# Ten gate blocks of each feed-forward: every second weight slab by seven block products over sums, and the feed-forward in two parts

## Chip, cores and metric

One core of a Trainium2 chip runs the whole program. The metric is the device time of one execution in microseconds, and a change counts by the ratio of the times of the kernel after and the kernel before, timed on the same chip. All numbers below are of the kernel before.

## What is computed

A sequence of 256 tokens with 2048 features (fp32) passes through a feed-forward, a token-mixing block, a second feed-forward, and two further layers. The change is in the two feed-forwards alone:

```
def _swiglu(h, w_gu, w_down):
    gate, up = jnp.split(h @ w_gu, 2, axis=-1)
    return (jax.nn.silu(gate) * up) @ w_down

x = x + 0.5 * _swiglu(_rmsnorm(x, ffn1_norm[l]), ffn1_w_gu[l], ffn1_w_down[l])
```

w_gu is 2048 x 11264 (5632 gate columns, then 5632 up columns), w_down is 5632 x 2048. The second feed-forward has the same shapes. Beside them runs the product of a 2048-vector with the 2048 x 6144 matrices w_ada of the two last layers: mod = silu(c) @ w_ada + b_ada.

## The kernel before

Weights come as **slabs**: 128 partitions x 1024 fp32 numbers (512 KB), which is two chunks of 128 rows of a weight matrix (WK = 2) by 512 of its columns (WN = 512). A product is computed to fp32 accuracy by splitting both operands into a high part (rounded to fp32r) and a low part (the rest), and adding three passes on TensorE: high x high, low tokens x high weights, high tokens x low weights. Tokens are the stationary operand (128 x 128, halves T = 0 and 1 of the 256 tokens), weights the moving one.

Each slab goes through five hands, on five queues:

1. SP issues its load into `stage`, a ring of RING = 4, once the slab four places earlier has been split.
2. ACT writes the high part into `split_slabs`, a ring of 4 (SPLIT_FFN), in slab order (`round_upto`, `rounded_part`, L1627). It waits for the load, and for `slab_done` of the slab four places earlier, whose place it takes.
3. POOL (`rest`, L880) or DVE (`slab_lo`, L2132) writes the low part, stage minus high part. The set `by_vector` says which: in a feed-forward about every second slab is DVE's.
4. PE multiplies (`wide_passes`): eight matmuls with the high part (L1088), then, after a wait for the low part, four with it (L1093), each 128 x 128 by 128 x 512. The last raises `slab_done`.
5. `slab_done` frees the place for ACT.

```
1088:  mm(ps[:, 2 * pair + T, :], stationary(kk, i)[:, T * P:(T + 1) * P], w[0][:, kk, :],
1090:  pe.wait_ge(*slab_split(n))
1093:  ins = mm(ps[:, 2 * pair + T, :], stationary(kk, 0)[:, T * P:(T + 1) * P], w[1][:, kk, :],
```

A feed-forward has 11 groups j of 16 slabs: eight for 512 gate columns, eight for the 512 up columns of the same place; then 4 groups d of 22 slabs of w_down. ACT takes the silu of the gate sums out of PSUM (L1696), DVE multiplies with the up sums (`gated`, L2172), turns the result by 32 x 32 blocks into PSUM (`turn_act`, L2186, 16 of them a group), ACT rounds it (`round_act`, L1702), and DVE writes its low part (`rest_act`, L2195). All of this is done one group behind, at fixed places q = 0 to 15 of the group.

DVE also computes the product with w_ada, 96 loads of two chunks in each feed-forward, at places `ADA_AT` between the slabs (`ada`): per load two multiply-adds over 128 x 512 (L2145 and L2149; the first of a column group is L2142), whose running sum `total` stands in PSUM, bank 5. Each eighth load ends with a transpose (L2152) and a sum (L2154).

The order on each engine is written out by hand as loops over groups and places; DVE, ACT, POOL and SP each work strictly through their own list, and meet only at semaphores.

## Time and profile before

| what | value |
|---|---|
| median of 3 runs | 3026.06 us (3023.61 to 3027.93) |
| the profiled execution, span | 3022.0 us, 46302 instructions |
| PE busy | 3001.6 us (99%), 18688 matmuls |
| DVE busy | 1983.5 us (66%) |
| ACT busy | 1449.2 us (48%) |
| POOL busy | 1326.5 us (44%) |
| first feed-forward | from 14 to 717 us of the span |
| second feed-forward | from 1447 to 2158 us of the span |

The profile gives for the profiled execution its span, from the first to the last instruction; no separate time of that execution is listed. The median of the runs is 4.1 us (0.13%) above the span. Busy time of an engine leaves out waits on semaphores, but contains the time in which an instruction that has begun is held up: that shows as a longer duration.

### The profile page before, as it was taken

The page shows a single profiled execution, that of the slowest core. Times are in us where ns is not written, and L with a number is a line of the kernel's source. Part 1 is how long each engine was busy: PE and PEld are TensorE (multiplying, and loading weights), DVE is VectorE, ACT ScalarE, POOL GpSimd, SP SyncE. Part 2 cuts the span into 40 slices and gives each one's busy share as a digit, 9 for nine tenths or more (in the row PEclk, how much of TensorE's full clock was granted, in tenths as well). Part 3 has the DMA queues.
Part 4 walks back from the last instruction along what each step waited for, and adds up shares of the span by engine and source line. Part 5 has one row for each costly group of instructions (what it writes and reads, how often), then busy time and mean ns, then how long its engine had stood idle before and what let it go on. Part 6 is the DMA issues. An engine that isn't in the chain of part 4 may idle for free.

```text
span 3022.0 us, 46302 instructions
## 1 busy us (share of the span) xinstructions
PE 3001.6 (99%) x18688; PEld 2660.7 (88%) x18688; DVE 1983.5 (66%) x2918; ACT 1449.2 (48%) x1885; POOL 1326.5 (44%) x653
## 2 busy tenths in 40 slices
PE   9999999999999999999999999999999999999998
PEld 7888888888999999998888888888899998999997
DVE  4777665664324457777566666577579866789764
ACT  6444444444657455544544444444544454544454
POOL 5455545445565555585554555444550004710013
PEclk9999999999999999999999999999999999999999
DMA  7888887886776555566688888788576546665555
GB/s 241 274 279 264 273 282 252 290 287 182 226 175 175 158 165 150 151 170 199 214 274 285 268 272 268 263 291 279 172 216 195 161 143 213 183 192 182 154 181 181
DMA packets 491662, 663.33 MB, mean 220 GB/s; under 512 B 70440, under 2 KB 278040, under 8 KB 490936
## 3 DMA queue, kind: packets, MB, share of 16 engines
q1 hardware_dynamic: 485960, 655.85, 68.5%
q0 software_dynamic: 4448, 2.94, 0.3%
q8 instruction: 147, 2.41, 0.3%
q10 hardware_dynamic: 1040, 1.58, 0.2%
q14 instruction: 67, 0.55, 0.1%
HBM read 656.06 MB, written 2.11 MB: 218 GB/s over the span
## 4 chain that ended last, share of the span: by engine, by line
PE 96%; DVE 3%; ACT 0%; issue 0%; POOL 0%; DMA 0%; DVEq 0%; ACTq 0%
PE ps L1088 37%; PE ps L952 20%; PE ps L1093 18%; PE ps L958 10%; PE ps L969 3%; PE ps L974 1%; PE ps L936 1%; DVE narrow_split_slabs L2132 1%; PE ps L1571 1%; PE ps L1350 1%; PE ps L1331 1%; DVE h_split L2089 1%; PE ps L1059 0%; DVE U L2082 0%; PE ps L1358 0%; PE ps L1388 0%
## 5 line engine op out<-in xcount | busy, mean ns | idle before, releaser
L880 POOL TENSOR_TENSOR split_slabs<-stage,split_slabs 128x1024 fp32r<-128x1024 f32 x318 | 775.4, 2439 | 1289.3 <-ACT split_slabs L1627 1289.2
L1627 ACT ACTIVATE split_slabs<-stage 128x1024 fp32r<-128x1024 f32 x592 | 627.3, 1061 | 858.7 <-PE ps L1093 790.8
L1088 PE MATMUL ps<-split_slabs,h_split 128*128 128x512 f32 x3288 | 813.1, 389 | 0.0
L1627 ACT ACTIVATE narrow_split_slabs<-stage 128x1024 fp32r<-128x1024 f32 (+1 forms) x437 | 457.7, 1051 | 611.0 <-PE ps L958 460.6
L1088 PEld LDWEIGHTS ps<-split_slabs,h_split 128*128 128x128 f32 x3288 | 616.9, 188 | 127.9
L2132 DVE TENSOR_TENSOR split_slabs<-stage,split_slabs 128x1024 fp32r<-128x1024 f32 x274 | 354.0, 1292 | 493.0 <-ACT split_slabs L1627 491.1
L952 PE MATMUL ps<-h_split,narrow_split_slabs 128*128 128x256 f32 x4928 | 620.6, 279 | 2.9 <-issue 1.9
L952 PEld LDWEIGHTS ps<-h_split,narrow_split_slabs 128*128 128x128 f32 x4928 | 586.0, 188 | 14.5 <-issue 8.7
L880 POOL TENSOR_TENSOR narrow_split_slabs<-stage,narrow_split_slabs 128x1024 fp32r<-128x1024 f32 (+1 forms) x182 | 441.2, 2434 | 317.5 <-ACT narrow_split_slabs L1627 317.1
L1093 PE MATMUL ps<-split_slabs,h_split 128*128 128x512 f32 x1644 | 439.4, 389 | 0.0
L2132 DVE TENSOR_TENSOR narrow_split_slabs<-stage,narrow_split_slabs 128x1024 fp32r<-128x1024 f32 x255 | 339.5, 1335 | 126.8 <-ACT narrow_split_slabs L1627 125.7
L1093 PEld LDWEIGHTS ps<-split_slabs,h_split 128*128 128x128 f32 x1644 | 308.6, 188 | 64.0
L1088 PE MATMUL ps<-split_slabs,act_split 128*128 128x512 f32 x1392 | 344.0, 389 | 0.0
L958 PE MATMUL ps<-h_split,narrow_split_slabs 128*128 128x256 f32 x2464 | 331.1, 277 | 0.0
L1088 PEld LDWEIGHTS ps<-split_slabs,act_split 128*128 128x128 f32 x1392 | 261.3, 188 | 54.1
L958 PEld LDWEIGHTS ps<-h_split,narrow_split_slabs 128*128 128x128 f32 x2464 | 303.7, 188 | 0.0
L1093 PE MATMUL ps<-split_slabs,act_split 128*128 128x512 f32 x696 | 186.0, 389 | 0.0
L2186 DVE STREAM_TRANSPOSE ps<-U 32x256 f32<-32x256 f32 x352 | 160.3, 455 | 4.9
L1093 PEld LDWEIGHTS ps<-split_slabs,act_split 128*128 128x128 f32 x696 | 130.7, 188 | 27.2
L2145 DVE SCALAR_TENSOR_TENSOR ps<-U,cact,ps 128x512 f32<-128x512 f32 x168 | 126.2, 751 | 14.8 <-DMA U<-in_w_ada 12.1
L2149 DVE SCALAR_TENSOR_TENSOR ps<-U,cact,ps 128x512 f32<-128x512 f32 x168 | 127.0, 756 | 6.0
L2568 DVE SCALAR_TENSOR_TENSOR U<-U,params 128x256 f32<-128x256 f32 x240 | 112.2, 509 | 0.0
(309 smaller groups left out, 2516.9 us busy)
## 6 DMA issues: line engine op xcount, KB each, us to landing
stage<-in_ffn_w_gu SPq DMA_DIRECT2D x352, 512.0 KB, 4.9
stage<-in_w_in SPq DMA_DIRECT2D x349, 512.0 KB, 3.9
U<-in_w_ada SPq DMA_DIRECT2D x192, 512.0 KB, 5.4
stage<-in_ffn_w_down SPq DMA_DIRECT2D x176, 512.0 KB, 5.1
stage<-in_w_out SPq DMA_DIRECT2D x96, 512.0 KB, 4.2
stage<-in_w_in SPq DMA_DIRECT2D x80, 128.0 KB, 2.8
stage<-in_w_branch_c SPq DMA_DIRECT2D x32, 192.0 KB, 3.5
stage<-in_cmp_w SPq DMA_DIRECT2D x8, 512.0 KB, 4.9
```

Source lines behind the costliest of these rows:

```text
L880: nc.gpsimd.tensor_tensor(slab_part(n, 1, size(n)), stage[:, n % RING, 0:size(n)], slab_part(n, 0, size(n)).bitcast(F32), ALU.subtract).th ...
L952: mm(bank[:, c * S:(c + 1) * S], w[0][:, kk, at:at + P], moving(kk, i), start=first and c == 0 and kk == 0 and i == 0, stop=False)
L958: ins = mm(bank[:, c * S:(c + 1) * S], w[1][:, kk, at:at + P], moving(kk, 0), start=False, stop=last and c == outs - 1 and kk == chunks - 1)
L969: mm(bank[:, T * W2:(T + 1) * W2], hx[:, i, KC * k + kk, T * P:(T + 1) * P], w[0][:, kk, :], start=k + T + kk + i == 0, stop=False)
L1088: mm(ps[:, 2 * pair + T, :], stationary(kk, i)[:, T * P:(T + 1) * P], w[0][:, kk, :], start=first and kk == 0 and i == 0, stop=False)
L1093: ins = mm(ps[:, 2 * pair + T, :], stationary(kk, 0)[:, T * P:(T + 1) * P], w[1][:, kk, :], start=False, stop=last and kk == WK - 1)
L1627: return fn(slab_part(n, 0, size(n)), stage[:, n % RING, 0:size(n)], ACT.Copy)
L2132: v.tensor_tensor(slab_part(n, 1), stage[:, n % RING, :], slab_part(n, 0).bitcast(F32), ALU.subtract).then_inc(lo_vec, 1)
L2145: ins = v.scalar_tensor_tensor(total, w[:, 0, :], cact[:, 2 * k:2 * k + 1], total, ALU.mult, ALU.add)
L2149: v.scalar_tensor_tensor(sums, w[:, 1, :], cact[:, 2 * k + 1:2 * k + 2], total, ALU.mult, ALU.add).then_inc(ada_load, 1)
L2186: last = v.transpose(dst[turned_rows, :, :, rows], src[rows, :, :, turned_rows])
L2568: ins = v.scalar_tensor_tensor(cy[:, c, :], src, col, cy[:, c, :], ALU.mult, ALU.add)
```

## The change

**The seven products.** In the groups j = 1 to 10 of both feed-forwards, of the eight gate slabs those with q = 1, 3, 5, 7 (STR_SLABS) are no longer multiplied directly. A slab of two chunks by 512 columns is seen as a 2 x 2 matrix of blocks of 128 x 256, the tokens of its two chunks as a 2 x 2 matrix of blocks of 128 x 128, and the product of the two is made by seven block products instead of eight (Winograd's form). Four of the seven take sums of weight blocks as the moving operand, and four take sums of token blocks as the stationary one.

- DVE (`sum_slab`) makes the weight sums: 128 x 512, then 128 x 256 twice, each from the one before, all from `stage` and `slab_sums` (which lies in the low part of the slab's place in the ring). It then also makes the low part of the three plain blocks (128 x 768).
- ACT makes two high parts: of the plain blocks (128 x 768, into the new ring `plain_split` of 2) and of the sums (128 x 1024).
- POOL makes the low part of the sums, as for any other slab.
- PE (`summed_passes`) multiplies 21 times 128 x 128 by 128 x 256, in four stretches with a wait before each, in place of 12 times 128 x 128 by 128 x 512.
- The seven products go to four PSUM banks (the gate pair and banks 4 and 5). Gate sums are therefore put together after the last slab: ACT copies a quarter (`copy_gate`, place 11), DVE adds three times and then once over 128 x 1024 (`sum_gate`, place 12), ACT takes the silu in SBUF (`silu_summed`, place 14).
- Once a feed-forward, in group 0, DVE and ACT make the token sums of the 8 chunks concerned, high and low part (`combine`, `round_combined`, `rest_combined`).

**Who makes the low parts.** In groups 1 to 10 DVE keeps two slabs of the sixteen (q = 10 and 15); the other fourteen are POOL's.

**The product with w_ada.** Its running sum moves from PSUM bank 5 to SBUF (`ada_run`), since bank 5 is taken. Six loads are placed in each of the ten groups (q = 2, 9, 11, 13, 14, 15), the remaining 36 in the down products.

**Two parts.** PARTS = ((0, 6), (6, 11)): after gate and up groups 0 to 5, the down product runs over their 24 chunks (4 groups of 12 slabs), and after groups 6 to 10 over the other 20 (4 groups of 10). x is thus updated eight times a feed-forward, not four. This halves the room for activations, which pays for the new tiles.

The core of the diff:

```
+PARTS = ((0, 6), (6, 11))
+ADA_SLABS = (2, 9, 11, 13, 14, 15)
+STR_SLABS = (1, 3, 5, 7)
...
+        by_vector -= {s + gu_at(j) + q for s in (S_F1, S_F2) for j in range(1, GU_GROUPS) for q in range(16)}
+        by_vector |= {s + gu_at(j) + q for s in (S_F1, S_F2) for j in range(1, GU_GROUPS) for q in (10, 15)}
...
+            def summed_passes(pair, n, q, first, last):
...
+                of_plain = ((tokens(0, 0), ps[:, 4, low]), (combined(3), ps[:, 2 * pair, low]), (tokens(1, 0), ps[:, 2 * pair, high]))
+                of_sums = ((combined(0), ps[:, 5, low]), (combined(1), ps[:, 5, high]), (combined(2), ps[:, 4, high]),
+                           (tokens(1, 1), ps[:, 2 * pair + 1, high]))
+                pe.wait_ge(plain_hi, nth_sum[n])
+                for k, (stationary, sums_to) in enumerate(of_plain):
+                    for i in range(2):
+                        mm(sums_to, stationary(i), whole[0][:, k, :], start=first and k == 0 and i == 0, stop=False)
+                pe.wait_ge(hi_done, nth[n])
...
+                pe.wait_ge(plain_lo, nth_sum[n])
...
+                pe.wait_ge(*slab_split(n))
...
+                    if m in nth_sum:
+                        k = nth_sum[m]
+                        act.wait_ge(*slab_loaded(m))
+                        if k > 2:
+                            act.wait_ge(slab_done, summed[k - 3] + 1)
+                        fn(plain_part(m, 0), stage[:, m % RING, STR_COLS:SLAB], ACT.Copy).then_inc(plain_hi, 1)
+                        act.wait_ge(slab_summed, k)
+                        fn(slab_part(m, 0), sums_of(m), ACT.Copy).then_inc(hi_done, 1)
...
-                w, total = u(ADA_RING, P, 2, WK, WN)[:, m % 2], ps[:, 5, :]
+                w, total = u(ADA_RING, P, 2, WK, WN)[:, m % 2], ada_run
...
+                def sum_slab(n):
+                    dve.wait_ge(*slab_loaded(n))
+                    dve.wait_ge(slab_done, before[n] + 1)
+                    whole, sums = col_blocks(stage[:, n % RING, :]), col_blocks(sums_of(n))
+                    chained(v.tensor_tensor(sums[:, 0:2, :], whole[:, 0:1, :].broadcast_to([P, 2, STR_COLS]), whole[:, 1:3, :], ALU.subtract), "sum1", n)
+                    chained(v.tensor_tensor(sums[:, 2, :], whole[:, 2, :], sums[:, 0, :], ALU.subtract), "sum2", n)
+                    v.tensor_tensor(sums[:, 3, :], whole[:, 3, :], sums[:, 2, :], ALU.subtract).then_inc(slab_summed, 1)
+                    dve.wait_ge(plain_hi, nth_sum[n])
+                    v.tensor_tensor(plain_part(n, 1), stage[:, n % RING, STR_COLS:SLAB], plain_part(n, 0).bitcast(F32), ALU.subtract
+                                    ).then_inc(plain_lo, 1)
...
+                def sum_gate(j):
+                    dve.wait_ge(gate_copied, (GU_GROUPS - 1) * f + j)
...
+                    v.tensor_tensor(u(SILU, P, TT, WN), u(SILU, P, TT, WN), ps[:, pair:pair + 2, :], ALU.add).then_inc(gate_summed, 1)
...
+                        if j > 0 and q == 12:
+                            sum_gate(j)
+                        if j == 0 and q == 11:
+                            combine()
+                        if j == 0 and q == 12:
+                            rest_combined()
...
+                for part, (j0, j1) in enumerate(PARTS):
+                    for j in range(j0, j1):
+                        gate_and_up(j)
+                    down(part)
```

How the order moves, first on PE, in the gate half of a group. Before, each slab is a row of eight matmuls with high parts and a row of four with low parts:

```order
L1088 MATMUL ps<-split_slabs,h_split 128x512 x8
L1093 MATMUL ps<-split_slabs,h_split 128x512 x4
L1088 MATMUL ps<-split_slabs,h_split 128x512 x8
L1093 MATMUL ps<-split_slabs,h_split 128x512 x4
```

After, an even slab (q = 0, 2, 4, 6) stays as it was (now L1153 and L1158), and an odd one reads:

```order
L1182 MATMUL ps<-plain_split,h_split 128x256 x2
L1182 MATMUL ps<-plain_split,combined_split 128x256 x2
L1182 MATMUL ps<-plain_split,h_split 128x256 x2
L1186 MATMUL ps<-split_slabs,combined_split 128x256 x6
L1186 MATMUL ps<-split_slabs,h_split 128x256 x2
L1189 MATMUL ps<-plain_split,h_split 128x256
L1189 MATMUL ps<-plain_split,combined_split 128x256
L1189 MATMUL ps<-plain_split,h_split 128x256
L1192 MATMUL ps<-split_slabs,combined_split 128x256 x3
L1192 MATMUL ps<-split_slabs,h_split 128x256
```

These are 14 matmuls with high parts and 7 with low parts, of half the width.

Second, on DVE, in the same half of a group, from `gated` on. Before (L2132 is a slab's low part, L2145 and L2149 are the product with w_ada, reading and writing PSUM):

```order
L2172 SCALAR_TENSOR_TENSOR U<-ps,rstd,U 128x512 x2
L2132 TENSOR_TENSOR split_slabs<-stage,split_slabs 128x1024
L2186 STREAM_TRANSPOSE ps<-U 32x2x4x32 x12
L2132 TENSOR_TENSOR split_slabs<-stage,split_slabs 128x1024
L2186 STREAM_TRANSPOSE ps<-U 32x2x4x32 x4
L2132 TENSOR_TENSOR split_slabs<-stage,split_slabs 128x1024
L2145 SCALAR_TENSOR_TENSOR ps<-U,cact,ps 128x512
L2149 SCALAR_TENSOR_TENSOR ps<-U,cact,ps 128x512
```

After (L2354 to L2358 are `sum_slab` of q = 3, 5 and, behind the first transposes, 7):

```order
L2322 SCALAR_TENSOR_TENSOR U<-ps,rstd,U 128x512 x2
L2354 TENSOR_TENSOR slab_sums<-stage 128x512
L2355 TENSOR_TENSOR slab_sums<-stage,slab_sums 128x256
L2356 TENSOR_TENSOR slab_sums<-stage,slab_sums 128x256
L2358 TENSOR_TENSOR plain_split<-stage,plain_split 128x768
L2354 TENSOR_TENSOR slab_sums<-stage 128x512
L2355 TENSOR_TENSOR slab_sums<-stage,slab_sums 128x256
L2356 TENSOR_TENSOR slab_sums<-stage,slab_sums 128x256
L2358 TENSOR_TENSOR plain_split<-stage,plain_split 128x768
L2336 STREAM_TRANSPOSE ps<-U 32x2x4x32 x8
```

The three low parts are gone from here, and each of the four odd slabs has four operations in their place. In the second half of the group the list reads, from place 9:

```order
L2295 SCALAR_TENSOR_TENSOR U<-U,cact 128x512
L2299 SCALAR_TENSOR_TENSOR U<-U,cact 128x512
L2282 TENSOR_TENSOR split_slabs<-stage,split_slabs 128x1024
L2295 SCALAR_TENSOR_TENSOR U<-U,cact 128x512
L2299 SCALAR_TENSOR_TENSOR U<-U,cact 128x512
L2345 TENSOR_TENSOR act_split<-ps,act_split 128x512 x2
L2388 TENSOR_TENSOR U<-U,ps 128x256
L2389 TENSOR_TENSOR U<-U,ps 128x2x256
L2390 TENSOR_TENSOR U<-U,ps 128x256
L2391 TENSOR_TENSOR U<-U,ps 128x1024
L2295 SCALAR_TENSOR_TENSOR U<-U,cact 128x512
L2299 SCALAR_TENSOR_TENSOR U<-U,cact 128x512
```

L2295 and L2299 are the product with w_ada, now from SBUF to SBUF; L2388 to L2391 are `sum_gate`.

## Rows read from the trace of the kernel before

**Rows 1.** The page's busy times: engine, busy us (share), instructions
```profile
PE 3001.6 (99%) x18688; PEld 2660.7 (88%) x18688; DVE 1983.5 (66%) x2918; ACT 1449.2 (48%) x1885; POOL 1326.5 (44%) x653
```
**Rows 2.** Waits, longest first (engine line <- releaser: us, times, longest), all engines
```profile
POOL split_slabs L880 <- ACT split_slabs L1627: 1289.2, 311, 235.3
ACT split_slabs L1627 <- PE ps L1093: 790.8, 517, 2.0
```
**Rows 3.** Timeline of PE, first feed-forward: start, us, engine line op operands xcount
```profile
302.43 1.98 PE L1088 MATMUL ps<-split_slabs,h_split 128*128 128x512 f32 x8
...
305.15 1.98 PE L1088 MATMUL ps<-split_slabs,h_split 128*128 128x512 f32 x8
```
**Rows 4.** Timeline of PE, token mixing, matmuls of half the width
```profile
797.34 1.98 PE L952 MATMUL ps<-h_split,narrow_split_slabs 128*128 128x256 f32 x16
...
800.06 1.98 PE L952 MATMUL ps<-h_split,narrow_split_slabs 128*128 128x256 f32 x16
```
**Rows 5.** Lines one by one: count, then duration ns min/median/max, first to last start
```profile
L880 POOL TENSOR_TENSOR split_slabs<-stage,split_slabs x318: 2357/2401/3400, 7.9 to 3003.5; 128x1024 fp32r<-128x1024 f32 x159
L2132 DVE TENSOR_TENSOR split_slabs<-stage,split_slabs x274: 1212/1226/3434, 24.2 to 3006.1; 128x1024 fp32r<-128x1024 f32 x137
L2145 DVE SCALAR_TENSOR_TENSOR ps<-U,cact,ps x168: 742/750/757, 78.2 to 2109.3; 128x512 f32<-128x512 f32 x168
L2149 DVE SCALAR_TENSOR_TENSOR ps<-U,cact,ps x168: 754/756/757, 77.3 to 2104.4; 128x512 f32<-128x512 f32 x168
L2460 DVE TENSOR_TENSOR U<-U x16: 692/1625/2194, 1301.7 to 1356.3; 128x512 f32<-128x512 f32 x16
```
**Rows 6.** The same view, operations of DVE that stay as they are
```profile
L2172 DVE SCALAR_TENSOR_TENSOR U<-ps,rstd,U x44: 737/744/753, 58.3 to 1922.5; 128x512 f32<-128x512 f32 x44
L2186 DVE STREAM_TRANSPOSE ps<-U x352: 440/456/468, 61.6 to 1936.5; 32x256 f32<-32x256 f32 x176
L2195 DVE TENSOR_TENSOR act_split<-ps,act_split x44: 680/683/686, 81.9 to 1947.9; 128x512 fp32r<-128x512 f32 x44
L2152 DVE STREAM_TRANSPOSE ps<-U x24: 727/727/728, 121.7 to 2110.8; 128x512 f32<-128x512 f32 x24
L2154 DVE TENSOR_REDUCE U<-ps x24: 691/692/693, 122.4 to 2111.6; 128x16 f32<-128x512 f32 x24
```
**Rows 7.** Timeline, ACT, DVE and POOL in a group: start, us [idle before <- releaser]
```profile
299.97 1.06 ACT L1627 ACTIVATE split_slabs<-stage 128x1024 fp32r<-128x1024 f32 x1 [0.51 <-PE ps L1093]
300.68 0.75 DVE L2145 SCALAR_TENSOR_TENSOR ps<-U,cact,ps 128x512 f32<-128x512 f32 x1
301.11 2.41 POOL L880 TENSOR_TENSOR split_slabs<-stage,split_slabs 128x1024 fp32r<-128x1024 f32 x1 [3.03 <-ACT split_slabs L1627]
301.47 0.76 DVE L2149 SCALAR_TENSOR_TENSOR ps<-U,cact,ps 128x512 f32<-128x512 f32 x1
```
**Rows 8.** Timeline, DVE and POOL overlapping in token mixing
```profile
1307.61 2.70 POOL L880 TENSOR_TENSOR narrow_split_slabs<-stage,narrow_split_slabs 128x1024 fp32r<-128x1024 f32 x1
1308.67 2.19 DVE L2460 TENSOR_TENSOR U<-U 128x512 f32<-128x512 f32 x1
1310.33 2.81 POOL L880 TENSOR_TENSOR narrow_split_slabs<-stage,narrow_split_slabs 128x1024 fp32r<-128x1024 f32 x1
```
**Rows 9.** Timeline, DVE and POOL overlapping in the first feed-forward
```profile
53.78 4.57 DVE L2132 TENSOR_TENSOR split_slabs<-stage,split_slabs 128x1024 fp32r<-128x1024 f32 x2
57.22 3.40 POOL L880 TENSOR_TENSOR split_slabs<-stage,split_slabs 128x1024 fp32r<-128x1024 f32 x1
...
186.87 2.40 POOL L880 TENSOR_TENSOR split_slabs<-stage,split_slabs 128x1024 fp32r<-128x1024 f32 x1 [3.04 <-ACT split_slabs L1627]
186.91 2.39 DVE L2291 TENSOR_SCALAR U<-U 128x32 f32<-128x32 f32 x1
```
**Rows 10.** Windows: us, busy (x) of PE, PEld, DVE, ACT, POOL, granted clock, DMA share, GB/s
```profile
104.30:479.30 375.00, 375.00 (x1656) 310.50 (x1655) 263.24 (x385) 165.44 (x174) 188.46 (x78) 1.00 0.82 273
845.00:855.00 10.00, 9.94 (x71) 9.79 (x71) 3.86 (x3) 4.02 (x5) 5.25 (x3) 0.83 0.77 157
```

309 lines of the change are left out of this document (215 added, 94 removed).

## Prediction

> **What bounds the kernel now.** I read the page's busy times first [rows 1]: PE is busy 99% of the span, and in a stretch of 375 us inside the first feed-forward all of it, at full granted clock [rows 10]. The waits say the same from the other side [rows 2]: ACT waits 517 times for PE to free a place, POOL 311 times for ACT; nobody keeps PE waiting. So what counts is the time that PE needs, and whether the others still keep up when PE needs less and they do more.
>
> **What PE saves.** One slab is 12 matmuls over 512 columns and takes 305.15 - 302.43 = 2.72 us [rows 3], 227 ns each. In token mixing, matmuls over 256 columns with the same roles (tokens stationary, weights moving) run 24 in 800.06 - 797.34 = 2.72 us [rows 4], 113 ns each: half the width costs half the time. A summed slab is 21 of these, 2.38 us, so 0.34 us less. Four a group, ten groups, two feed-forwards: 80 x 0.34 = 27 us. A group of 16 slabs goes from 43.5 us to 42.2 us of PE.
>
> **What DVE gets.** Two SBUF inputs over 512 columns take 692 ns undisturbed (L2460's minimum), over 1024 columns 1226 ns (L2132's median) [rows 5], so 1.04 ns a column and 158 ns fixed: 256 columns 0.42, 768 columns 0.96 us. In one of the ten groups DVE has:
> - four `sum_slab`: 4 x (0.69 + 0.42 + 0.42 + 0.96) = 10.0 us;
> - two low parts: 2 x 1.23 = 2.5 us;
> - six loads of w_ada: 6 x (0.75 + 0.76) = 9.1 us [rows 5];
> - unmoved work [rows 6]: `gated` 2 x 0.74, transposes 16 x 0.456, `rest_act` 2 x 0.68, three quarters of a fold (0.73 + 0.69), together 11.2 us; and `sum_gate`, 0.42 + 0.69 + 0.42 + 1.23 = 2.8 us.
>
> That is 35.6 us in 42.2: it would fit, if each operation took what it takes alone. ACT has 12 x 1.06 + 4 x (1.06 + 0.8) + some 3 us for silu, rounding and copy, about 23 us: no bound. POOL has 14 low parts x 2.40 = 33.7 us, where it had 78 in 375 us, nine a group [rows 10]. Each fits alone. The question is whether DVE and POOL fit beside each other.
>
> **They don't, in the trace.** A DVE operation with one input in SBUF and one in PSUM runs through POOL's low part untouched: L2149 starts at 301.47 inside POOL's 301.11 to 303.52 and takes 0.76 [rows 7], and of 168 the longest took 757 ns [rows 5]. One with both inputs in SBUF is held: L2460 begins at 1308.67 while POOL works from 1307.61 to 1310.31, and ends at 1310.86, 2.19 us in place of 0.69; and POOL's next one, begun at 1310.33, takes 2.81 in place of 2.41 [rows 8]. With 1024 columns, the second L2132 of the pair in [rows 9] is behind POOL until 57.2, and the next POOL operation takes 3.40. Even a small TENSOR_SCALAR from SBUF to SBUF took 2.39 us beside POOL's 2.40. The kernel before lives with it since few of DVE's operations are of this kind there: the median of L2132 is the undisturbed one, as DVE and POOL take turns. The change makes nearly all of them such: the sums read `stage` and `slab_sums`, and the product with w_ada, until now safe in PSUM, has its sum in SBUF.
>
> The Trainium skill, SBUF — State Buffer, "Who interferes with whom", says that a DVE instruction with two SBUF inputs contends with a GpSimd instruction that reads SBUF, and that the pair of ports is held for the full instruction, the other one blocking. By whole durations that would be 33.7 + 21.6 = 55.3 us a group, and +216 us in all; the trace agrees that they exclude one another, but its pair of 0.69 and 2.41 takes 2.82 us, not 3.10 [rows 8], so the sums below are smaller.
>
> **The sum for a group.** What excludes one another: POOL's 33.7 us and DVE's 10.0 + 2.5 + 9.1 = 21.6 us. A DVE operation between two of POOL's saves 0.69 + 2.41 - 2.82 = 0.28 us of that, at most 14 times: 33.7 + 21.6 - 3.9 = **51.4 us**, against 42.2 us of PE. That packs both lists without a hole. In their fixed orders they have holes: POOL can't start an odd slab's low part before DVE's three sums and ACT's rounding, and DVE, in that time, arrives at operations that POOL holds up. Going once through DVE's list in order with these durations, I find eleven operations that meet a low part of POOL under way, mean wait 1.7 us (half of 2.4, and more where POOL goes in between two chained sums). That gives 35.6 + 11 x 1.7 = **54 us**, DVE being the longest list. From below: if the lock cost only what POOL is seen to lose (0.41 us for 512 columns, 1.0 for 1024, by the same line 0.1 for 256 and 0.7 for 768), a group would be 33.7 + 4 x 1.3 + 2 x 1.0 + 12 x 0.41 = **46 us**. I take 53, between the first two and nearer to the ordered one.
>
> **The lead.** POOL is now early: the slab whose place ACT fills from 299.97 has its low part at 303.52 [rows 7], and PE reaches it three slabs on, and its low passes 1.8 us later, at about 309.7. Each run of five groups starts with this lead of 6 us, and the down products behind it, where POOL and DVE keep to alternate slabs, give it back. There are four such runs. A run: 5 x 53 = 265 us of DVE and POOL against 5 x 42.2 = 211 of PE, less 6: 48 us of new waiting for PE, less the 5 x 1.36 = 7 us that PE saves: +41. Four runs: +165 us.
>
> **Edits of small cost.** Token sums, once a feed-forward: 2048 columns (2.3 us), 4 x 0.69, and a low part over 2048 (2.3), 7.4 us on DVE with both inputs in SBUF, in front of low parts that PE wants; the lead covers most, I take 3 us each, bounds 0 and 9: +6. Parts: eight more updates of x in all (1.3 us each on DVE, PE going on in the other pair of banks): nothing, while DVE is under half busy there; and the last activations of a part are wanted at slab 10 or 8 of the down product, not 20, while DVE makes them at place 9, about a slab ahead of PE's need: nothing, up to 2 us each if late, 8 in all. Places of w_ada in the down products fall in turn with POOL's low parts, as before: nothing. A place in `stage` is free only when POOL is through, so loads start later as well; that follows POOL's pace and adds nothing to it.
>
> **Forecast.** 165 + 6 = +171 us on the profiled span of 3022.0, which gives 3193; the median of the runs is 4 us above that span, so **3197 us**.
>
> **Rivals.**
> - *Slots fit, faster.* Sums and the w_ada product fall into POOL's waits, as L2132 does now, and PE never waits: 3026 - 27 + 6 = 3005. For it: POOL has 1289 us of waits now [rows 2]. Against it: the 8.5 us that POOL has left in a group of 42.2 would have to hold 21.6 us of DVE. It decides once DVE's share on the shared path is under 10 us a group. 0.07.
> - *Soft lock.* 46 us a group: 5 x 46 - 211 - 6 - 7 = +6 a run, +24 and +6: 3056. For it: POOL's 3.40 and 2.81. Against it: DVE's own list, in which these waits are then spent. 0.15.
> - *The clock.* PE now has pauses. In a stretch in token mixing in which it was 9.94 of 10 us busy, the mean granted clock was 0.83 [rows 10], so some 3.4 us at the lower level, 1.2 GHz, at a price of 1.7 us. Once a group that is up to +34 us: 3231. The Trainium skill, TensorE: Matmul & The Clock Gate, "HAM oscillation", says that waits between bursts of matmuls can bring the clock down again and again; no row here shows more than the one fall. Against it: in my walk through the lists PE's pauses are 0.5 to 2 us long, with matmuls between. 0.08.
> - The forecast itself: 0.67. The rest, 0.03, is the change giving about nothing.
>
> **Numbers.** A measurement of this kernel can tell 0.2%, 6 us, from no change. Faster 0.07, same 0.03, slower 0.90. Range: down to the soft lock, 3055; up to 54 us a group (+20), late activations (+8) and half the clock's price (+17), 3245. It leaves out the faster case and what is above.
>
> **What would show it.** Right: low parts of POOL at a mean of 2.7 to 2.9 us; the product with w_ada at 1.2 to 1.8 us an operation in place of 0.75, and the sums likewise, with single ones up to 3 us; PE waiting for POOL's low parts and for high parts that wait for sums, 6 to 11 us in a group, and PE 93 to 95% busy; groups 50 to 54 us long; the down products at 2.72 us a slab as before; token mixing and the layers unchanged. The 21 half-width matmuls at 2.4 us a slab where nothing is late. Wrong: undisturbed medians on DVE beside a POOL that is 80% busy, or groups under 46 us.

## The result, and the profile after

| | before | after |
|---|---|---|
| median | 3025.11 us of 4 (3023.61 to 3027.93) | 3309.97 us of 4 (3307.93 to 3311.2) |
| ratio, 95% interval | | 1.0939 [1.0924, 1.0955] |
| profiled span | 3022.0 us | 3308.1 us |
| mean granted clock | 0.998 | 0.986 |

The change costs 285 us, where the prediction said 171 and let the range end at 3245 us. The direction, the mechanism and the main place were as forecast. The size was not, and an eighth of the cost lies in the down products, where the prediction had nothing.

The busy times on the page, and the shares by engine in the chain that ended last, of the changed kernel:

```profile
PE 3087.2 (93%) x19408; PEld 2701.9 (82%) x19408; DVE 2602.1 (79%) x3236; ACT 1507.2 (46%) x1987; POOL 1640.6 (50%) x755
PE 48%; DVE 34%; DMA 7%; issue 7%; ACT 2%; POOL 1%; SPq 0%; DVEq 0%; ACTq 0%
```

Against [rows 1] DVE has 619 us more of busy time for 318 more instructions, and PE waits. In the chain DVE now holds a third of the span. Where the time lies is seen in a table by stage. It is worked out from the starts of PE's slabs: from the first matmul of one group of 16 slabs (or one down product) to the first of the next; the last down product of a feed-forward is taken to the start of its last matmul. "Part 1" and "part 2" are groups 0 to 5 and 6 to 10 with their down products; before there was one down product over all 44 chunks.

| us | before | after, first feed-forward | after, second |
|---|---|---|---|
| group 0 | 48.5 and 44.4 | 54.7 | 47.8 |
| groups 1 to 5 | 43.5 each | 53.1, 58.1, 58.7, 58.7, 58.0 | 50.9, 55.7, 55.9, 56.0, 55.8 |
| down product, part 1 | (part 2 included) 239.6 | 131.3 | 131.1 |
| groups 6 to 10 | 43.5 each | 51.6, 55.8, 57.0, 56.3, 57.2 | 48.4, 55.9, 56.0, 56.3, 57.1 |
| down product, part 2 | | 27.9, 30.2, 33.4, 34.4 | 27.9, 28.8, 35.1, 33.8 |
| whole feed-forward | 723.4 and 719.4 | 876.5 | 852.6 |

The twenty groups take 241.9 us more, the two groups 0 take 9.6, the down products 34.7: 286.2 us, and nothing elsewhere (the spans differ by 286.1). The forecast had 165, 6 and 0.

Windows over groups 2 and 3 of the second feed-forward, first of the changed kernel, then two groups' length of the same stage before (columns as in rows 10):

```profile
1694.30:1805.90 111.60, 93.93 (x457) 74.94 (x457) 105.42 (x112) 43.75 (x50) 73.70 (x29) 0.98 0.61 208
```

```profile
1540.00:1627.00 87.00, 87.00 (x386) 72.06 (x385) 58.37 (x84) 38.23 (x40) 43.24 (x19) 1.00 0.83 272
```

A group is 55.8 us; in it DVE is busy 52.7 us and idle 3.1, POOL is busy 36.9, PE 47.0. DVE has taken PE's place as the engine that is always busy. How it fills 52.7 us with a list of 35 is in the lines, of the changed kernel (line, engine, operation, operands, count | busy us, mean ns | idle before):

```profile
L2299 DVE SCALAR_TENSOR_TENSOR U<-U,cact 128x512 f32<-128x512 f32 x192 | 284.0, 1479 | 6.8
L2295 DVE SCALAR_TENSOR_TENSOR U<-U,cact 128x512 f32<-128x512 f32 x168 | 205.9, 1226 | 32.6 <-DMA U<-in_w_ada 29.5
L2282 DVE TENSOR_TENSOR split_slabs<-stage,split_slabs 128x1024 fp32r<-128x1024 f32 x172 | 299.9, 1745 | 134.2 <-ACT split_slabs L1738 133.9
L2354 DVE TENSOR_TENSOR slab_sums<-stage 128x512 f32<-128x512 f32 x80 | 121.8, 1522 | 20.4 <-DMA stage<-in_ffn_w_gu 20.1
L2356 DVE TENSOR_TENSOR slab_sums<-stage,slab_sums 128x256 f32<-128x256 f32 x80 | 79.6, 995 | 2.8
L2355 DVE TENSOR_TENSOR slab_sums<-stage,slab_sums 128x256 f32<-128x256 f32 x80 | 79.4, 993 | 2.8
L2358 DVE TENSOR_TENSOR plain_split<-stage,plain_split 128x768 fp32r<-128x768 f32 x80 | 75.9, 949 | 0.0
...
L945 POOL TENSOR_TENSOR split_slabs<-stage,split_slabs 128x1024 fp32r<-128x1024 f32 x340 | 895.5, 2648 | 1054.5 <-ACT split_slabs L1738 1054.5
L945 POOL TENSOR_TENSOR split_slabs<-slab_sums,split_slabs 128x1024 fp32r<-128x1024 f32 x80 | 198.3, 2479 | 203.0 <-ACT split_slabs L1751 203.0
```

The product with w_ada took 750 and 756 ns an operation while its sum was in PSUM [rows 5]; it takes 1226 and 1479 on average now. The first weight sum has 1522 ns in place of 0.69 us, the two narrow ones 0.99 in place of 0.42. Only the 128x768 low part (L2358) is undisturbed: it follows at once on the sums for which POOL's next operation waits, and none of the 80 begins while POOL is at work. Of the 80 first sums (L2354), 50 begin under an operation of POOL's, and just these 50 are longer than the shortest (678 ns) by more than 150 ns. Some of these meetings in full, first DVE's timeline in the first feed-forward, and then POOL's operation that it meets:

```profile
209.87 2.77 DVE L2299 SCALAR_TENSOR_TENSOR U<-U,cact 128x512 f32<-128x512 f32 x1
212.56 3.42 DVE L2282 TENSOR_TENSOR split_slabs<-stage,split_slabs 128x1024 fp32r<-128x1024 f32 x1
215.89 2.87 DVE L2295 SCALAR_TENSOR_TENSOR U<-U,cact 128x512 f32<-128x512 f32 x1
218.80 2.77 DVE L2299 SCALAR_TENSOR_TENSOR U<-U,cact 128x512 f32<-128x512 f32 x1
221.50 1.27 DVE L2345 TENSOR_TENSOR act_split<-ps,act_split 128x512 fp32r<-128x512 f32 x2
```

```profile
212.04 2.85 POOL L945 TENSOR_TENSOR split_slabs<-stage,split_slabs 128x1024 fp32r<-128x1024 f32 x1
```

Four operations in a row of DVE, 3.5 us of work by themselves, fill 11.7 us: the first ends at 212.64, 0.6 us after POOL's next one began at 212.04, and the second begins under that one and ends 1.1 us after it; then `act_split`, with an input in PSUM, takes 0.64 us each. And the cost reaches PE: of its waits in the changed kernel the largest are

```profile
PE ps L1192 <- POOL split_slabs L945: 57.5, 65, 1.2
PE ps L1153 <- ACT split_slabs L1738: 53.5, 28, 3.5
...
PE ps L1186 <- ACT split_slabs L1751: 43.5, 43, 4.1
...
PE ps L1158 <- DVE split_slabs L2282: 36.9, 28, 4.5
```

and behind ACT's stand DVE and the loads, in the same view:

```profile
ACT split_slabs L1751 <- DVE slab_sums L2356: 337.2, 80, 8.1
ACT split_slabs L1738 <- DMA stage<-in_ffn_w_gu: 225.3, 92, 6.1
```

In [rows 2] ACT waited for PE, as one does who feeds the bound. Now it waits for a sum of DVE's, or for a slab that was loaded late (SP's own longest wait, 757 us in 212 pieces, is for POOL's low parts, which free a place in `stage`).

### The profile page after: what moved, and what is told of

Its sections match the earlier page's. It is cut to its first block, busy times and chain, and to the rows that moved or that the text cites. A ratio compares the mean times of both kernels' runs of the same rounds, so it can differ in the third digit from the quotient of the medians.

```text
span 3308.1 us, 48355 instructions
## 1 busy us (share of the span) xinstructions
PE 3087.2 (93%) x19408; PEld 2701.9 (82%) x19408; DVE 2602.1 (79%) x3236; ACT 1507.2 (46%) x1987; POOL 1640.6 (50%) x755
## 3 DMA queue, kind: packets, MB, share of 16 engines
q8 instruction: 153, 2.51, 0.3%
## 4 chain that ended last, share of the span: by engine, by line
PE 48%; DVE 34%; DMA 7%; issue 7%; ACT 2%; POOL 1%; SPq 0%; DVEq 0%; ACTq 0%
PE ps L1017 18%; PE ps L1023 9%; PE ps L1153 7%; DVE U L2299 6%; DVE U L2295 5%; DVE ps L2336 4%; PE ps L1158 4%; DVE slab_sums L2354 4%; DMA stage<-in_ffn_w_gu 3%; DMA stage<-in_ffn_w_down 2%; PE ps L1034 2%; DVE slab_sums L2355 2%; DVE plain_split L2358 2%; DVE slab_sums L2356 2%; DVE split_slabs L2282 2%
## 5 line engine op out<-in xcount | busy, mean ns | idle before, releaser
L945 POOL TENSOR_TENSOR split_slabs<-stage,split_slabs 128x1024 fp32r<-128x1024 f32 x340 | 895.5, 2648 | 1054.5 <-ACT split_slabs L1738 1054.5
L1738 ACT ACTIVATE split_slabs<-stage 128x1024 fp32r<-128x1024 f32 x512 | 535.4, 1056 | 580.8 <-DMA stage<-in_ffn_w_gu 225.3
L1153 PE MATMUL ps<-split_slabs,h_split 128*128 128x512 f32 x2648 | 680.7, 400 | 35.8 <-ACT split_slabs L1738 35.8
L1153 PEld LDWEIGHTS ps<-split_slabs,h_split 128*128 128x128 f32 x2648 | 502.7, 193 | 150.0 <-issue 35.8
L2282 DVE TENSOR_TENSOR split_slabs<-stage,split_slabs 128x1024 fp32r<-128x1024 f32 x172 | 299.9, 1745 | 134.2 <-ACT split_slabs L1738 133.9
L1158 PE MATMUL ps<-split_slabs,h_split 128*128 128x512 f32 x1324 | 367.7, 400 | 30.5 <-DVE split_slabs L2282 23.7
L1153 PE MATMUL ps<-split_slabs,act_split 128*128 128x512 f32 x1392 | 350.4, 395 | 17.7 <-ACT split_slabs L1738 17.7
L1158 PEld LDWEIGHTS ps<-split_slabs,h_split 128*128 128x128 f32 x1324 | 241.4, 189 | 113.3 <-DVE split_slabs L2282 35.1
L1153 PEld LDWEIGHTS ps<-split_slabs,act_split 128*128 128x128 f32 x1392 | 264.6, 191 | 76.4 <-issue 11.4
L945 POOL TENSOR_TENSOR split_slabs<-slab_sums,split_slabs 128x1024 fp32r<-128x1024 f32 x80 | 198.3, 2479 | 203.0 <-ACT split_slabs L1751 203.0
L2299 DVE SCALAR_TENSOR_TENSOR U<-U,cact 128x512 f32<-128x512 f32 x192 | 284.0, 1479 | 6.8
L1751 ACT ACTIVATE split_slabs<-slab_sums 128x1024 fp32r<-128x1024 f32 x80 | 84.8, 1060 | 337.2 <-DVE slab_sums L2356 337.2
L2295 DVE SCALAR_TENSOR_TENSOR U<-U,cact 128x512 f32<-128x512 f32 x168 | 205.9, 1226 | 32.6 <-DMA U<-in_w_ada 29.5
L1158 PE MATMUL ps<-split_slabs,act_split 128*128 128x512 f32 x696 | 190.3, 396 | 14.4 <-DVE split_slabs L2282 13.2
L1158 PEld LDWEIGHTS ps<-split_slabs,act_split 128*128 128x128 f32 x696 | 131.7, 191 | 45.8 <-DVE split_slabs L2282 15.3
```

The source lines that it names most:

```text
L945: nc.gpsimd.tensor_tensor(slab_part(n, 1, size(n)), whole, slab_part(n, 0, size(n)).bitcast(F32), ALU.subtract).then_inc(lo_pool, 1)
L1738: return fn(slab_part(n, 0, size(n)), stage[:, n % RING, 0:size(n)], ACT.Copy)
L1751: fn(slab_part(m, 0), sums_of(m), ACT.Copy).then_inc(hi_done, 1)
L2282: v.tensor_tensor(slab_part(n, 1), stage[:, n % RING, :], slab_part(n, 0).bitcast(F32), ALU.subtract).then_inc(lo_vec, 1)
L2295: ins = v.scalar_tensor_tensor(total, w[:, 0, :], cact[:, 2 * k:2 * k + 1], total, ALU.mult, ALU.add)
L2299: v.scalar_tensor_tensor(sums, w[:, 1, :], cact[:, 2 * k + 1:2 * k + 2], total, ALU.mult, ALU.add).then_inc(ada_load, 1)
```

## The experiments

Theory **A**, the prediction's: DVE's operations with both inputs in SBUF and POOL's low parts exclude one another, and DVE's list, with what it is held, sets the length of a group. Rival **B**: DVE and POOL would do, but more work, more steps in ACT's order or the half-width matmuls cost the time by themselves. Rival **C**: the parts (and what was moved with them) carry a good share. Stage lengths are taken as in the table above. Diffs are against the changed kernel unless another one is named.

**e1_pool_memset: POOL without reads**

```diff
                 pool.wait_ge(hi_done, nth[n])
+                if n in in_groups:
+                    nc.gpsimd.memset(slab_part(n, 1, size(n)).bitcast(F32), 0.0).then_inc(lo_pool, 1)
+                    return
```

> In groups 1 to 10 POOL fills the low parts with zeros (one write of 128 x 1024) and reads nothing from SBUF; the low part of those 14 weight slabs is left out of the product. DVE, ACT, PE and SP do what they do in the changed kernel. Theory A (DVE and POOL exclude one another when both read SBUF, and that alone makes DVE's list longer than PE's): sums at 0.69 and 0.42 us, the w_ada product at 0.75, DVE's list of 35.6 us fits in a group of 42.2 us, groups at 42 to 44 us, in all 3035 to 3060 us (the last down products stay slow). Rival B (DVE's list with its chain through sums, ACT's rounding and the gate sums is too long by itself): groups stay at 55 us, 3290 to 3310.

Measured: 3047.89 us, ratio 1.0077 [1.0047, 1.0106], 262 us under the changed kernel. Every wait and every order is as in it; only POOL's fourteen operations a group read nothing, and the low parts of these slabs are zeros. POOL's lines and DVE's sums, and the window over groups 2 and 3 of the second feed-forward:

```profile
L946 POOL MEMSET split_slabs<- 128x1024 f32 x280 | 268.1, 958 | 577.4 <-ACT split_slabs L1742 289.1 <-ACT split_slabs L1755 283.6
...
L2358 DVE TENSOR_TENSOR slab_sums<-stage 128x512 f32<-128x512 f32 x80 | 55.2, 690 | 61.1 <-PE ps L1196 30.6 <-PE ps L1162 26.7 <-DMA stage<-in_ffn_w_gu 3.5
```

```profile
1543.90:1629.50 85.60, 85.60 (x457) 74.19 (x456) 68.79 (x112) 44.77 (x50) 26.88 (x28) 1.00 0.81 270
```

All twenty groups take 42.8 us, PE is busy in all of it, and DVE needs 34.4 us of busy time a group: 18.3 us less than in the changed kernel. That is what it is held. DVE's durations added one by one give 35.4 us a group, where the prediction had 35.6. Of the 80 first sums, 21 run beside a memset of POOL's, and the longest of all 80 took 695 ns. (POOL is also shorter here, 0.96 us for 2.4. POOL was idle for 19 us of a group in the changed kernel, so its own list was not the bound; but a low part is also ready sooner, and no run has an operation of POOL's that lasts 2.4 us and reads nothing. The 18.3 us are read from DVE's own durations; that all of the 262 us come of them isn't shown apart from this.) Rival B falls for the groups: with 21 matmuls a slab, all of ACT's steps and all waits in place, PE never stops there.

The same run shows two costs outside the contention in the groups. The first: PE saves less than forecast. Its timeline over one summed slab, from 195.19 to 197.70:

```profile
195.19 0.40 PE L1186 MATMUL ps<-plain_split,h_split 128*128 128x256 f32 x2
195.42 0.40 PE L1186 MATMUL ps<-plain_split,combined_split 128*128 128x256 f32 x2
195.66 0.40 PE L1186 MATMUL ps<-plain_split,h_split 128*128 128x256 f32 x2
195.90 0.88 PE L1190 MATMUL ps<-split_slabs,combined_split 128*128 128x256 f32 x6
196.62 0.40 PE L1190 MATMUL ps<-split_slabs,h_split 128*128 128x256 f32 x2
...
197.58 0.28 PE L1196 MATMUL ps<-split_slabs,h_split 128*128 128x256 f32 x1
197.70 2.00 PE L1157 MATMUL ps<-split_slabs,h_split 128*128 128x512 f32 x8
```

Two matmuls take 0.24 us, 120 ns each, where those of [rows 4] are 113 ns apart: 2.51 us a slab, 0.21 under a plain one and not 0.34. So a group goes from 43.5 to 42.8 us, and twenty save 14 us, not 27. The second: groups 0 (+6.8 and +3.4) and the down products (+12.2 and +15.5) stay as long as this without any contention in the groups. The sum, -14 + 10.2 + 27.7 = +24, is the whole difference of this run's span to that of before (3046.1 against 3022.0). (In the down products POOL reads as before, so the operations there still meet.) Even with the contention in the groups gone, the change loses.

**e2_ada_short: a shorter product with w_ada**, over 32 of its 512 columns (the opening operation of each column group stays at 512; of the others only those of one load in each feed-forward do, the eighth, where the expectation says every eighth):

```diff
                 w, total = u(ADA_RING, P, 2, WK, WN)[:, m % 2], ada_run
+                cols = slice(0, WN if m == 7 else 32)
...
-                    ins = v.scalar_tensor_tensor(total, w[:, 0, :], cact[:, 2 * k:2 * k + 1], total, ALU.mult, ALU.add)
+                    ins = v.scalar_tensor_tensor(total[:, cols], w[:, 0, cols], cact[:, 2 * k:2 * k + 1], total[:, cols], ALU.mult, ALU.add)
```

> The product with w_ada is taken over 32 of 512 columns (all loads stay, and every eighth load in full), so most of it is left out. Theory A: what excludes one another falls from 51.4 to about 43 us a group, and with holes groups come to 46 to 48 us; the down products of the second part return to 27 to 28 us; in all 3080 to 3130 us. Rival B (length of DVE's list alone): DVE loses 12 x 0.55 = 6.6 us a group, groups at 49 us, 3170 us. If SP's queue, where a w_ada load holds up slab loads until DVE has used the one two before, is what counts, the gain is as large as under A, but ACT's waits for slab loads vanish as well.

Measured: 3215.55 us, ratio 1.0631 [1.0597, 1.0665], 94 us under the changed kernel, above the ranges of theory A and of rival B. One of its lines (two of its 192 are over 512 columns), and that of the first narrow sum, in the same view as above:

```profile
L2300 DVE SCALAR_TENSOR_TENSOR U<-U,cact 128x32 f32<-128x32 f32 x192 | 142.8, 744 | 6.9
...
L2356 DVE TENSOR_TENSOR slab_sums<-stage,slab_sums 128x256 f32<-128x256 f32 x80 | 98.2, 1227 | 2.8
```

A sixteenth of the columns, and still half of the mean time (744 ns; 1479 in the changed kernel). Groups 7 to 10 of the second feed-forward take 51.8 to 53.7 us. The twelve operations of a group are each some 0.5 us shorter by themselves, 6 us together, and those groups gained 3 to 4; the first narrow sum meanwhile got longer (1227 ns where it had 993). What an operation waits for when it meets POOL is the rest of POOL's, whatever its own size: the number of meetings counts, not the columns. That can be counted. Take as held each operation of DVE's that is more than 150 ns longer than the shortest of its line and shape: in the second feed-forward's groups 1 to 10 of the changed kernel these are 10 to 12 a group, 17.6 to 22.1 us together; with the short product they are 9 to 11, 15.2 to 19.9 us. My reading that the cost goes with the length failed here.

**e3_parts: the parts alone**, with the silu of before and without the sums' steps on ACT and DVE:

```diff
-        by_vector -= {s + gu_at(j) + q for s in (S_F1, S_F2) for j in range(1, GU_GROUPS) for q in range(16)}
-        by_vector |= {s + gu_at(j) + q for s in (S_F1, S_F2) for j in range(1, GU_GROUPS) for q in (10, 15)}
-        summed = [s + gu_at(j) + q for s in (S_F1, S_F2) for j in range(1, GU_GROUPS) for q in STR_SLABS]
+        summed = []
...
-                w, total = u(ADA_RING, P, 2, WK, WN)[:, m % 2], ada_run
+                w, total = u(ADA_RING, P, 2, WK, WN)[:, m % 2], ps[:, 5, :]
```

> The two parts alone: no summed slab, low parts shared between POOL and DVE as before, the running sum of the w_ada product in PSUM bank 5, its places those of the changed kernel. The prediction's step: parts cost nothing, at most 8 us: 3025 to 3033. Rival: the down products of the second part, ten slabs for transposes of x, its update, low parts and w_ada, are over DVE's capacity by themselves: they take 30 to 35 us each as in the changed kernel, 3050 to 3060.

Measured: 3053.86 us, ratio 1.0096 [1.0067, 1.0126]. All groups from 1 on take 43.5 us, as before; the down products of part 1 take 32.6 each, those of part 2 27.2, 27.2, 29.2, 35.3 and 27.2, 28.8, 33.2, 35.5 us (10 slabs of 2.72 are 27.2). So C is right in kind: the parts cost 29 us here, 25 of them in the last two or three down products of each feed-forward. DVE's timeline where the last of them begins, first feed-forward:

```profile
699.54 0.76 DVE L2291 SCALAR_TENSOR_TENSOR ps<-U,cact,ps 128x512 f32<-128x512 f32 x1
700.33 1.80 DVE L2189 STREAM_TRANSPOSE h_plain<-x_res 32x256 f32<-32x256 f32 x4
...
705.99 5.97 DVE L2172 SCALAR_TENSOR_TENSOR h_split<-h_plain,params,h_split 128x256 fp32r<-128x256 f32 x4
...
714.81 3.38 DVE L2274 TENSOR_TENSOR split_slabs<-stage,split_slabs 128x1024 fp32r<-128x1024 f32 x2
718.12 1.21 DVE L2398 SCALAR_TENSOR_TENSOR x_res<-ps,x_res 128x1024 f32<-128x1024 f32 x1
```

DVE has the next stage's transposes and splits, the update of x and the product with w_ada in one place, and a low part that PE wants stands behind them: between 705.99 and 714.81 DVE makes none. This too is in part the exclusion: of the four splits at 705.99 two take 2.62 us each, beside POOL's low parts of 705.84 and 708.69, and two take 0.47, so 4.3 of the 5.97 us are waiting, and the first of the two late low parts takes 2.25 in place of 1.23. PE's wait for such a low part, which is its longest sum here:

```profile
PE ps L1156 <- DVE split_slabs L2274: 11.9, 3, 5.1
```

Before, the last down product had 22 slabs for that list, now 10.

**e4_parts_ada: the same, with w_ada's sum in SBUF** (against e3_parts)

```diff
-                w, total = u(ADA_RING, P, 2, WK, WN)[:, m % 2], ps[:, 5, :]
+                w, total = u(ADA_RING, P, 2, WK, WN)[:, m % 2], ada_run
```

> As the run with the parts alone, but with the running sum of w_ada in SBUF, as in the changed kernel. Theory A: in the groups what excludes one another is 8 x 2.4 + 8 x 1.2 + 9.1 - 2 = 36 us of 43.5, so groups hold or lose a microsecond; where DVE is full (down products of the second part) it costs 5 to 15 us in all. 3030 to 3060, and at least 5 us above the run with the parts alone. Rival (the move of the sum is free): the same time as parts alone.

Measured: 3058.7 us (3053.08 and 3064.33), ratio 1.0112 [1.0067, 1.0158]; the profiled spans with and without are 3051.3 and 3050.8 us. These runs tell no difference, where I had expected one. All groups from 1 on take 43.5 us. Here POOL makes nine low parts of the sixteen and DVE seven, two or three of DVE's operations are held in nearly every group (at most one in e3), and DVE is still idle for 5 us or more: it has time to be held. In these groups the move of the sum costs nothing by itself; what it costs beside fourteen low parts of POOL's and the weight sums is seen only together with its places (e13, below).

**e5_ada_psum4: four summed slabs, w_ada's sum in PSUM**

```diff
-    early = [gu_at(j) + q for j in range(1, GU_GROUPS) for q in ADA_SLABS]
+    early = [gu_at(j) + q for j in range(1, GU_GROUPS) for q in (12, 13, 14, 15, 16, 17, 18, 20)]
+    return early + [down_at(0) + 12 + 2 * i for i in range(16)]
...
-                        if ADA_AT[m] == i:
+                        if ADA_AT[m] + 1 == i:
...
+                if m % 8 == 0 and lows_done[0]:
+                    dve.wait_ge(act_lo, lows_done[0])
...
-                w, total = u(ADA_RING, P, 2, WK, WN)[:, m % 2], ada_run
+                w, total = u(ADA_RING, P, 2, WK, WN)[:, m % 2], ps[:, 7, :]
```

> All four summed slabs a group as in the changed kernel, POOL with 14 low parts, but the product with w_ada back in PSUM: its running sum in bank 7, whole column groups of eight loads at places 12 to 15 of a group and 0 to 4 of the next, when the transposed activations don't need that bank; the last down products are free of it. DVE's operations with both inputs in SBUF fall from 29 a group to 18. Theory A: what excludes one another is 33.7 + 12.5 - 3.9 = 42.3 us a group, DVE's own list 39 us and some 7 meetings with POOL at 1.4 us: groups at 46 to 49 us; last down products at 27 to 28 us; in all 3080 to 3140 us. Rival (each meeting with POOL costs so much that only their number on the sums counts): groups stay above 50 us, over 3160.

Measured: 3249.02 us, ratio 1.0745 [1.0724, 1.0767], far above theory A's 3080 to 3140. The product is back at 754 and 756 ns an operation and DVE's busy time is down, but a group of the second feed-forward still takes 53 us. The window over its groups 2 and 3, and DVE's new waits:

```profile
1657.30:1762.80 105.50, 91.85 (x457) 75.40 (x457) 83.78 (x120) 43.76 (x51) 69.09 (x29) 0.98 0.72 239
```

```profile
DVE ps L2299 <- DMA U<-in_w_ada: 145.5, 105, 4.1
DVE ps L2296 <- issue: 119.8, 20, 8.0
```

DVE is busy for 41.9 us of 52.8 and waits for the rest. Only three to six operations a group are held now, 4.4 to 11.1 us together. The PSUM bank used is free only in a stretch of a group, so eight loads of w_ada stand in nearly consecutive places, through a ring of two: DVE waited 105 times for one, and all that is behind it on DVE waited too. The second line, 119.8 us in 20 pieces, is another matter: it stands before the first load of each eight, whose place in the ring had long been free. Once, DVE's row and SP's:

```profile
1697.87 0.76 DVE L2296 TENSOR_SCALAR ps<-U,cact 128x512 f32<-128x512 f32 x1 [6.40 <-issue]
```

```profile
1692.55 0.37 SPq L839 DMA_DIRECT2D stage<-in_ffn_w_gu  x1
1692.96 0.47 SPq L848 DMA_DIRECT2D U<-in_w_ada  x1
```

DVE was through with what stands before at 1691.5. SP issued the load only at 1692.96, behind that of a slab whose place POOL freed at 1692.54; it landed at 1697.78, and L2296 began at 1697.87. In this run SP issues each load of w_ada one place later than in the changed kernel (`ADA_AT[m] + 1`), so DVE waits for POOL's pace over SP's queue as well. One bound was taken away and a second one built, of two parts: close loads, and loads issued late.

**e8_parts_places: the parts with those places of w_ada, no sums.** The edit is that of e3_parts with the first five changed lines of e5_ada_psum4.

> The parts alone, sums of w_ada in PSUM as in the run of the parts alone, but with the places of the w_ada product changed: eight loads a group, 16 in the down products of the first part, none in the second part's. If the 29 us of the parts are DVE's full list in the last down products, they vanish: 3022 to 3030 us. Rival: they are the shorter time from the last activations to their use, or the transposes of x: 3045 to 3055 as before.

Measured: 3040.51 us, ratio 1.0058 [1.0043, 1.0073], 13 us under e3_parts. The last three down products of part 2 take 27.2, 27.2 and 27.6 us in both feed-forwards (the first 33.3 and 34.9). With no w_ada in the last products, e3's loss there is gone. In the groups DVE waits for the close loads here too, with the same late issue and nine low parts of POOL's beside it, and 18 of the 20 groups take 43.5 us all the same (the others 43.7 and 45.1):

```profile
DVE ps L2285 <- DMA U<-in_w_ada: 172.3, 127, 3.7
```

So that wait costs time only where DVE's list has no room for it.

**e9_two_later and e10_three_later: two and three summed slabs, from group 2 on, otherwise as e5_ada_psum4.** In e10 STR_SLABS is (3, 5, 7) and DVE keeps 1, 10 and 15; in both the token sums are made in group 1, in six steps.

```diff
-STR_SLABS = (1, 3, 5, 7)
+STR_SLABS, COMB_SLABS = (3, 7), (1, 3, 5, 7)
...
+        by_vector |= {s + gu_at(j) + q for s in (S_F1, S_F2) for j in range(2, GU_GROUPS) for q in (1, 10, 13, 15)}
```

> Two summed slabs (q = 3 and 7) a group from group 2 on, four low parts of sixteen on DVE, w_ada in PSUM, and the token sums spread over the places of group 1. What excludes one another is 12 x 2.4 + 5.0 + 4.9 - 3.4 = 35 us of 43: PE should not wait. A summed slab saves 2.72 - 2.53 = 0.19 us where nothing waits, so 36 x 0.2 = 7 us in all: 3017 to 3025 us. If the meetings still bind: above 3035.

> The same with three summed slabs (q = 3, 5 and 7) and three low parts on DVE. What excludes one another: 13 x 2.4 + 7.5 + 3.7 - 3.6 = 39 us of 42.9. Without waiting 54 x 0.2 = 11 us saved: 3014 us. I expect some waiting in the first half of the group, where POOL has eight low parts less one in 20.5 us: 3015 to 3060.

Measured: 3187.98 us, ratio 1.0542 [1.0518, 1.0567], and 3215.71 us, ratio 1.0638 [1.0621, 1.0654]. With more than half of e5's sums gone (36 left of 80), only 61 of its 226 us over the kernel before went with them. DVE's waits in e9_two_later:

```profile
DVE ps L2299 <- DMA U<-in_w_ada: 137.5, 92, 3.5
DVE ps L2296 <- issue: 107.6, 19, 6.5
```

They are those of e5, nearly as large: they belong to the eight loads close together and issued late, not to the sums. My expectation had missed this second bound.

**e12_carry2, e14_carry3, e13_carry4: six spread loads.** So that the loads can be spread again, w_ada's sum stands in PSUM within a group's stretch and is carried in SBUF from one stretch to the next: of a group's twelve operations one reads it from SBUF and one writes it there. There are six loads a group again, not eight, and SP issues them at their own place again, not one later. e12 has the summed slabs of e9, e14 those of e10, e13 those of the change.

```diff
+ADA_WINDOW = (12, 14, 15, 17, 18, 20)
...
+    early = [gu_at(j) + q for j in range(1, GU_GROUPS) for q in ADA_WINDOW]
+    return early + [down_at(0) + 10 + 36 * i // 26 for i in range(26)] + [down_at(1) + 10 + 14 * i // 10 for i in range(10)]
...
-                    ins = v.scalar_tensor_tensor(total, w[:, 0, :], cact[:, 2 * k:2 * k + 1], total, ALU.mult, ALU.add)
+                    ins = v.scalar_tensor_tensor(bank, w[:, 0, :], cact[:, 2 * k:2 * k + 1], ada_run if opens else bank, ALU.mult, ALU.add)
...
-                sums = ada_total if k == 7 else total
+                sums = ada_total if k == 7 else ada_run if closes else bank
```

> Two summed slabs a group from group 2 on, as in the run before with two, but six loads of w_ada a group at places 12, 14, 15 and 1, 2, 4 of the next, with the running sum in PSUM bank 7 inside this window and carried over once a group in SBUF; 26 loads in the down products of the first part, 10 in the first two of the second. That run with two had DVE idle 10 us a group, waiting for w_ada loads at eight places in a row with a ring of two. If that was what bound it, groups fall from 51 to 43 to 44 us and the whole to 3018 to 3040 us. If meetings of DVE and POOL bound it, groups stay above 47 us, over 3080.

> The same with three summed slabs from group 2 on. If meetings are few, PE saves 0.2 us a slab: 3015 to 3035 us; if the first half of the group is where they bind, groups at 45 to 47 us, 3050 to 3090.

> All four summed slabs a group from group 1 on, POOL with 14 low parts, as in the changed kernel; only the w_ada product is changed: in PSUM inside a window, carried over once a group in SBUF, spread as in the run above. DVE's operations with both inputs in SBUF fall from 29 to 19 a group. DVE's list 38 us alone, plus some 5 to 8 us of waiting for POOL (4 us were measured with eight loads in a row): groups at 44 to 48 us, 3060 to 3130 us. If the lock of the sums alone binds: groups at 50 us or more, above 3170.

| | summed slabs in all | median us | ratio | groups 6 to 10, second feed-forward |
|---|---|---|---|---|
| e12 | 36 | 3056.29 | 1.0105 [1.0089, 1.0120] | 43.2, 43.2, 45.9, 45.6, 44.0 |
| e14 | 54 | 3098.58 | 1.0233 [1.0213, 1.0254] | 43.4, 47.1, 46.8, 47.8, 46.8 |
| e13 | 80 | 3133.21 | 1.0359 [1.0338, 1.0380] | 44.5, 47.8, 47.9, 47.6, 48.8 |

e13 has all the sums of the change and lies 177 us under it: so much comes from w_ada's sum in SBUF and from its places (by the stage lengths 152 us in the groups and 29 in the down products, where no w_ada stands at the end). The window over groups 2 and 3 of the second feed-forward, and the weight sums' line, of e13_carry4:

```profile
1596.70:1690.50 93.80, 88.22 (x458) 74.13 (x457) 83.79 (x111) 44.06 (x51) 70.21 (x29) 1.00 0.73 245
```

```profile
L2367 DVE TENSOR_TENSOR slab_sums<-stage 128x512 f32<-128x512 f32 x80 | 134.0, 1675 | 11.7 <-DMA stage<-in_ffn_w_gu 7.5 <-PE ps L1159 3.7
```

DVE is busy 41.9 us a group, as in e5, but the group takes 46.9 and not 52.8: 5.9 us for six spread loads, issued earlier, in place of eight close ones; these three changes weren't made one by one. In the groups of this window seven and six operations are held, 8.3 and 8.1 us together; a part of it is the first weight sum, 1675 ns in the mean and 690 alone. At each step from 36 to 80 summed slabs the time rises. POOL's low parts rise with them, from 12 to 13 and 14 a group, so that the sums' own share isn't separated from POOL's. All three are above what I expected: e12 above 3018 to 3040 (few meetings), e14 above 3015 to 3035 and by 9 us above 3050 to 3090, e13 by 3 us above 3060 to 3130.

**e15_parts_early: the parts with those spread places, no sums** (against e3_parts)

```diff
-    early = [gu_at(j) + q for j in range(1, GU_GROUPS) for q in ADA_SLABS]
+    early = [gu_at(j) + q for j in range(1, GU_GROUPS) for q in (12, 14, 15, 17, 18, 20)]
+    return early + [down_at(0) + 10 + 36 * i // 26 for i in range(26)] + [down_at(1) + 10 + 14 * i // 10 for i in range(10)]
```

> No summed slab; the parts alone, w_ada in PSUM, with the places of the two runs above: none in the last two down products of the second part, six loads a group with gaps. If DVE's full list in those down products was the price of the parts, 3022 to 3032 us; the run with the parts alone had 3054, the one with eight loads in a row 3041.

Measured: 3031.41 us in the median of ten runs, ratio 1.0029 [1.0011, 1.0048]; the down products of part 2 take 27.2, 27.2, 27.2, 27.6 and 27.2, 28.3, 30.0, 28.4 us. The parts' 29 us are down to 8 with w_ada out of the last two down products. One of the ten took 3056.99, the others 3028 to 3035. This is the fastest of all the versions with parts, and it has no summed slab; none beat the kernel before.

## Why the prediction was right and wrong

**The mechanism and the main place: right.** 262 of the 285 us go when POOL reads nothing in the groups (e1). Three of the four down products of part 1 run at 2.72 us a slab, and outside the feed-forwards nothing changed. Operations with w_ada take 1.23 and 1.48 us in the mean (1.2 to 1.8 said), single sums over 2.4 us (up to 3 said), POOL's low parts 2.65 (2.7 to 2.9 said, so just under it), and PE is idle for 8.8 us of a group (6 to 11 said). Rival B fell with e1, where it speaks of the groups; C is true for a tenth of the loss (e3) to an eighth (the down products of the change).

**What DVE is held: right.** 54 - 35.6 = 18.4 us a group forecast, 52.7 - 34.4 = 18.3 measured. Nor is that luck: the walk through the list in order had eleven meetings of 1.7 us, and the trace has 10 to 12 a group, 1.6 to 1.9 us each in the mean. The Trainium skill, SBUF — State Buffer, "Who interferes with whom", names the same exclusion, and e1 agrees: 18.3 us of DVE's busy time a group go when POOL's operation no longer reads.

**The step that failed: "I take 53, between the first two and nearer to the ordered one".** It makes a group as long as DVE's list and DVE's waiting for POOL, and puts all other idle time of DVE at nothing. DVE is in fact busy for 52.7 us, but a group takes 55.8 in the second feed-forward and up to 58.7 in the first. Of the 115 us between 171 and 286, 77 are in the groups (242 for 165), 4 in group 0 (9.6 for 6) and 35 in the down products. Three things are in the groups' 77:
- The choice itself. 51.4 us is what the shared path needs if it is never free, and the fixed orders leave holes: in groups 3 and 8 of the second feed-forward POOL, or an operation of DVE's with no operand in PSUM, is at work in 51.2 to 51.5 of 56 us. So that sum was right for the path and too low for a group; the ordered walk's 54 was the better one.
- DVE as the bound isn't busy all the time. It is idle for 3.1 us a group: the waits seen are for slabs and w_ada loaded late (L2354 and L2295 wait for DMAs) and for high parts of ACT's. The prediction said that late loads follow POOL's pace and add nothing. They add where DVE has no time to lose.
- Small operations. In the first feed-forward four to six on 128x32 stand in each of groups 2 to 5, two of them held. They were missing in the list of unmoved work, though [rows 9] showed such a row. DVE is busy for 54.5 to 55.7 us in these groups, for 51.8 to 53.7 in those of the second feed-forward, and they are 2 to 3 us longer. DVE's timeline in group 3:

```profile
179.43 0.18 DVE L2503 TENSOR_TENSOR U<-U 128x32 f32<-128x32 f32 x1
179.65 0.18 DVE L2504 TENSOR_SCALAR U<-U 128x32 f32<-128x32 f32 x1
179.86 2.39 DVE L2503 TENSOR_TENSOR U<-U 128x32 f32<-128x32 f32 x1
182.29 2.30 DVE L2504 TENSOR_SCALAR U<-U 128x32 f32<-128x32 f32 x1
```

With the mean of groups 2 to 5 (or 7 to 10) of each run in place of 53, the prediction's own formula, 5 x group - 211 - 6 - 7, gives +68 and +59 in the first feed-forward, +55 and +58 in the second: +240 us, and 241.9 were measured. So the rest of the formula held.

**"Parts: nothing, while DVE is under half busy there": failed.** 29 us alone (e3), 35 in the change, where the bound was 8. The prediction counted the updates of x and the last activations, and took the places of w_ada in the down products as harmless, "as before". It didn't see that the last products of a feed-forward have 10 slabs each where there were 22, while the next stage's transposes and splits in them are as many as before. It is DVE's list again, with operations held by POOL in it, and moving w_ada away mends most of it (e8, e15).

**"PE saves 27 us": the size was off, 14 measured.** The pace was taken from a stretch with 113 ns a matmul; these go at 120 (e1). It has no part in the miss: where DVE sets the length of a group, the 7 us a run that PE saves cancel against the 211 that it needs. Group 0: 6.2 and 3.4 us, forecast 3 each, inside the bounds of 0 and 9.

**The lead: right.** The first group of each run is 5 to 8 us shorter than the next but one; 6 was said.

**The range.** Its upper terms, 20 + 8 + 17 over 3197, add up to 3242, not 3245; the measured time is outside either.

**The rivals.** *Slots fit* fell: PE is idle for 8.8 us of a group, and 50 of 80 first sums met POOL. *Soft lock* fell: the groups it puts at 46 us took 55.8. *The clock* is there, in part. The windows of the changed kernel in the first feed-forward:

```profile
100.00:200.00 100.00, 83.34 (x389) 68.80 (x388) 92.69 (x105) 35.37 (x41) 58.19 (x24) 0.90 0.58 193
200.00:300.00 100.00, 83.79 (x392) 67.14 (x392) 95.10 (x104) 38.19 (x44) 62.66 (x25) 0.95 0.63 212
```

PE is busy 83 and 84 of 100 us, in stretches with pauses between them, and the mean granted clock is 0.90 and 0.95: some of the time at the lower level, 1.2 GHz, where before it was 1.00 in this stretch [rows 10]. In the second feed-forward it is 0.96 to 1.00 by group. DVE is busy 93 and 95 us of the hundred, which speaks for PE having waited longer had it been faster, and the longer groups here go with longer busy time of DVE, as said above. No run takes the clock's share apart; e14, at a mean of 0.998 over the program, still had most groups at 46 to 49 us.

**Open, not tried:** why half-width matmuls go 120 ns apart in summed slabs and 113 in [rows 4]; how much of e5's waits a ring of more than two for w_ada would save, and how much issuing the loads at their old place; and what a lower share of POOL's with all four sums would bring.

## What to carry to other kernels

Before an engine gets more work "since it is half idle", list which of its operations exclude one another with its neighbour's long ones, and count the meetings, not the columns: here each cost the rest of the neighbour's operation. Where such an engine becomes the bound, the ordered walk through its list is the floor, and its waits for loads and for other engines come on top (3.1 us of 55.8 here). Read the price of a saving from the very operations that will run, and weigh it against all that makes room for it: seven products for eight gave 0.7 us of 43.5 here, 14 in all, and the parts and group 0 with its token sums cost 38 even without the exclusion in the groups (e1).

## What the runs showed of the hardware beyond that

- An operation's size hardly matters when it meets POOL's: on DVE 128x32 from SBUF to SBUF took 0.18 us undisturbed and up to 2.39, as long as POOL's whole low part. It is the start that decides: of the first sums and the operations with w_ada, 168 of 440 began under a low part of POOL's, and 167 of these were held.
- A POOL memset of 128x1024 took 0.96 us, and DVE's sums with two inputs in SBUF took at most 695 ns, the 21 of 80 that ran beside it too.
- Matmuls of 128x128 by 128x256 went 120 ns apart in summed slabs and 113 in token mixing, both at full granted clock.
